# Output projection of a hybrid decoder block: two of its four column chunks in one seven-product block

## The reference

```
merged = sigmoid(ga) * y_attn + sigmoid(gc) * y_conv      # 256 x 2048
mix    = merged @ w_out                                   # w_out is 2048 x 2048
h      = layer_norm(DN_ALPHA * h + mix, ln2_g, ln2_b)
```

## Time and profile before

| | us |
|---|---|
| median of 3 runs | 2113.2 |
| lowest and highest run | 2110.99, 2113.87 |
| span of the profiled execution (first to last instruction) | 2109.5 |
| TensorE matmul busy | 2095.7 (99%) |
| VectorE busy | 1877.2 (89%) |
| ScalarE busy | 1402.9 (67%) |

### The profile page before, as it was taken

One profiled execution on the slowest core, in us unless ns is written; L12 is line 12 of the kernel. 1 busy time (PEld: TensorE's weight loads), 2 busy tenths in 40 slices (PEclk: granted clock), 3 DMA queues, 4 the chain that ended last, 5 costly groups with the idle time before them and its releaser, 6 DMA issues.

```text
span 2109.5 us, 23778 instructions
## 1 busy us (share of the span) xinstructions
PE 2095.7 (99%) x9386; PEld 1734.6 (82%) x9386; DVE 1877.2 (89%) x1420; ACT 1402.9 (67%) x1313; POOL 216.7 (10%) x345
## 2 busy tenths in 40 slices
PE   9999999999999999999999999999999999999998
PEld 7888888888888888888888888888888888888886
DVE  7899999999996889999999986659899999999996
ACT  6677777777775546766676445335677777777773
POOL 0111111101110001011100000000111111100110
PEclk9999999999999999999999999999999999999999
DMA  9798988888985759998898556755788988899892
GB/s 369 253 295 260 279 270 266 291 300 277 289 279 231 276 158 311 299 269 270 304 301 262 212 185 240 260 178 200 244 294 255 282 272 267 290 302 278 288 285 113
DMA packets 92397, 556.65 MB, mean 264 GB/s; under 512 B 13056, under 2 KB 13440, under 8 KB 35200
## 3 DMA queue, kind: packets, MB, share of 16 engines
q1 hardware_dynamic: 68544, 437.69, 54.7%
q0 software_dynamic: 23744, 117.46, 25.8%
HBM read 534.13 MB, written 20.97 MB: 263 GB/s over the span
## 4 chain that ended last, share of the span: by engine, by line
PE 88%; DVE 8%; DMA 2%; ACT 1%; issue 1%; SPq 0%; DVEq 0%; ACTq 0%
PE acc L2259 14%; PE acc L2261 14%; PE acc L2260 14%; PE tb L2259 12%; PE tb L2261 12%; PE tb L2260 12%; PE acc L2197 3%; PE acc L2199 3%; PE acc L2198 3%; DVE g_lo L1338 3%; DVE cacc L1777 3%; DMA g_raw<-in_groups 1%; PE tb L2245 1%; DVE w_lo L1315 1%; DVE g_raw L1346 1%
## 5 line engine op out<-in xcount | busy, mean ns | idle before, releaser
L1338 DVE TENSOR_TENSOR g_lo<-g_raw,g_hi 128x2048 fp32r<-128x2048 f32 x506 | 1147.6, 2286 | 120.4 <-ACT g_hi L817 119.8
L817 ACT ACTIVATE g_hi<-g_raw 128x2048 fp32r<-128x2048 f32 x506 | 964.4, 1916 | 319.8 <-DVE g_raw L1346 121.5
L2259 PE MATMUL acc<-g_hi,xF_hi 128*128 128x512 f32 x1184 | 464.3, 392 | 0.6 <-ACT acc L899 0.6
L2261 PE MATMUL acc<-g_hi,xF_lo 128*128 128x512 f32 x1184 | 461.1, 389 | 0.0
L2260 PE MATMUL acc<-g_lo,xF_hi 128*128 128x512 f32 x1184 | 460.7, 389 | 0.0
L2259 PE MATMUL tb<-g_hi,xF_hi 128*128 128x512 f32 x760 | 296.3, 390 | 0.3 <-DVE g_lo L1338 0.2
L2261 PE MATMUL tb<-g_hi,xF_lo 128*128 128x512 f32 x760 | 295.7, 389 | 0.0
L2260 PE MATMUL tb<-g_lo,xF_hi 128*128 128x512 f32 x760 | 295.7, 389 | 0.0
L1346 DVE TENSOR_TENSOR g_raw<-g_raw,g_raw 128x2048 f32<-128x2048 f32 x120 | 274.3, 2286 | 1.3
L2259 PEld LDWEIGHTS acc<-g_hi,xF_hi 128*128 128x128 f32 x1184 | 222.3, 188 | 46.8 <-ACT acc L899 1.0
L2261 PEld LDWEIGHTS acc<-g_hi,xF_lo 128*128 128x128 f32 x1184 | 222.2, 188 | 46.8
(11 more groups left out here) (180 smaller groups left out, 2307.7 us busy)
## 6 DMA issues: line engine op xcount, KB each, us to landing
g_raw<-in_groups SPq DMA_DIRECT2D x356, 1024.0 KB, 7.2
g_raw<-in_groups POOLq DMA_DIRECT2D x80, 1024.0 KB, 8.6
raw<-in_stream SPq DMA_DIRECT2D x80, 512.0 KB, 4.5
bounce<-h_sq POOLq DMA_DIRECT2D x40, 256.0 KB, 5.5
h_in<-bounce POOLq DMA_DIRECT2D x160, 64.0 KB, 2.6
ln_gb<-in_ln SPq DMA_DIRECT2D x6, 1024.0 KB, 6.6
g_raw<-in_groups SPq DMA_DIRECT2D x6, 512.0 KB, 9.7
res<-in_x_rows SPq DMA_DIRECT2D x1, 2048.0 KB, 16.6
```

The lines of the kernel that those rows point to most:

```text
L817: act.activation(g_hi[:, n % RING], source[:], ACT.Copy).then_inc(g_hi_ready, 1)
L1338: dve.tensor_tensor(g_lo[:, n % RING], source[:], f32(g_hi[:, n % RING]), ALU.subtract).then_inc(g_lo_ready, 1)
L2259: pe.matmul(bank, x_hi_ap, g_hi[:, n % RING, blk], start=begin, stop=False, skip_group_check=True)
L2261: return pe.matmul(bank, x_lo_ap, g_hi[:, n % RING, blk], start=False, stop=end, skip_group_check=True)
```

## The change

The output projection's four column chunks are handled in another form. Chunk 0 and chunk 3 stay plain; chunks 1 and 2 become one seven-product block between them (chunk 1 in the place of "u", chunk 2 in the place of "g"). All weights come as 1 MB groups through `g_raw`, in the same numbering as the rest of the kernel, and units remain only for the two projections ahead of it.

- The block has 14 product groups and no plain groups among them. T1a, T1b, T2a and T2b are made by VectorE; T3a, T3b, T4a and T4b by adding DMAs from GpSimd.
- The factor sums S1 to S4 are made from two raw quarters, which ScalarE now copies out of PSUM when column blocks 0 and 1 are transposed (`merged_hi`, c < 2, four more copies), and from two that are still in PSUM.
- The plain chunk 0 accumulates in banks 2 and 3 (Z and W of the block), chunk 3 as well. So P5a, which opens bank W, waits until VectorE has taken chunk 0 out of both banks (`plain_rows`).
- Seven `g_raw` places are in use in this stage, three of them new (8 to 10; 8 and 9 lie over the convolution's factors). The loads of the norm's gain and bias now wait for P7b, and the second feed-forward's first loads stand behind them in SyncE's queue.
- Rows of the pair: `u_rows` (scale and subtract, then add a bank) and `g_rows`; statistics of all chunks are taken while the last chunk runs.

The diff, cut to the tables, the orders of the engines and the new waits:

```diff
+OUT_PAIR = ("P1a", "P1b", "P5a", "P5b", "P6a", "P3a", "P6b", "P3b", "P7a", "P7b", "P2a", "P2b", "P4a", "P4b")
+OUT_LOADS = {"qa": "P4a", "qb": "P4b", "ra": "P7a", "rb": "P7b", "ua": "P3a", "ub": "P3b", "ga": "P2a", "gb": "P2b"}
...
+OUT_SUMS = ("T1a", "T1b", "T2a", "T2b")
+OUT_PLAIN = (0, 3)
+OUT_U, OUT_G = 1, 2
...
+    def output(self, n, sums):
+
+        self.begin["out"] = (n, len(self.order))
+        n = self.output_plain(n, 0)
+        self.number("out", 0, True)
+        for m, name in enumerate(OUT_PAIR):
+            self.at["out", 0, name] = n + m
+        for name, last in OUT_LOADS.items():
+            self.load_at["out", 0, name] = len(self.order)
+            matrix, p = WEIGHTS[name]
+            self.load("out", (OUT_G, OUT_U)["gu".index(matrix)] * COLS, p, self.at["out", 0, last])
...
+            if k == outs:
+                free = {x: n - 7 for n, x in enumerate((4, 5, 10, 0, 1, 8, 9))}
...
+            slot_free(KO, 4)
+            load_group(KO)
+            sp.wait_ge(tr_full, t_convt + 4)
+            load_group(KO + 1)
+            load_group(KO + 2)
+            sp.wait_ge(lo_ready, UNITS - 2)
+            load_group(KO + 3)
+            sp.wait_ge(lo_ready, UNITS)
+            load_group(KO + 4)
+            sp.wait_ge(unit_used, UNITS)
+            for k in range(KO + 5, K1):
+                load_group(k)
+            sp.wait_ge(g_used, G.at["out", 0, "P7b"] + 1)
             load_gb(1, ln_gb[1])
-            for k in range(K1, K1 + 2):
+            for k in range(K1, K2):
+                if k in G.behind_out:
+                    sp.wait_ge(g_used, N1)
...
+                split_loaded(f, g, "P1a", "qa")
+                split_loaded(f, g, "P1b", "qb")
+                factors_hi(f)
+                split_sum(f, g, "P5a", "qa", "T1a")
+                fork(f, g, acc[:, BY], acc[:, BX], "P1b")
+                split_sum(f, g, "P5b", "qb", "T1b")
+                split_sum(f, g, "P6a", "qa", "T2a")
+                split_loaded(f, g, "P3a", "ua")
+                act.wait_ge(acc_out[1], 2 * (u1_end + 1))
+                fork(f, g, acc[:, BZ], acc[:, BW], "P5b")
+                split_sum(f, g, "P6b", "qb", "T2b")
+                split_loaded(f, g, "P3b", "ub")
+                act.wait_ge(t3a_ready, 16 * BLOCKS)
+                split(f, g, "P7a", "ra")
+                act.wait_ge(t3b_ready, fulls(f, g))
+                split(f, g, "P7b", "rb")
+                save_out(0, "P6b")
+                split_loaded(f, g, "P2a", "ga")
+                split_loaded(f, g, "P2b", "gb")
+                save_out(1, "P7b")
+                act.wait_ge(t4a_ready, fulls(f, g))
+                split(f, g, "P4a", "qa")
+                act.wait_ge(t4b_ready, 16 * (BLOCKS + 1))
+                split(f, g, "P4b", "qb")
...
-            hi(mix_out, 0, 4, 5, 6, 7)
+            split_out(0, 2)
             merged_hi(3)
-            with act.Fori(1, ND) as i:
-                hi(mix_out, i, *range(UD))
+            split_out(0, 3)
+            out_pair()
+            for p in range(PIECES):
+                split_out(1, p)
...
+            def plain_rows(m, t):
+
+                if m and t == 0:
+                    dve.wait_ge(out_full, 1)
+                else:
+                    dve.wait_ge(g_used, G.first["out", m] + PIECES)
+                cols = slice(OUT_PLAIN[m] * COLS, (OUT_PLAIN[m] + 1) * COLS)
+                dve.scalar_tensor_tensor(out=res[:, t, cols], in0=res[:, t, cols], scalar=ALPHA, in1=acc[:, 2 + t],
+                                         op0=ALU.mult, op1=ALU.add).then_inc(acc_out[1], 1)
...
+                bank, n, behind = ((BZ, 2, "P3b"), (BW, 3, "P5b"))[t]
+                dve.wait_ge(forked, forks("out", 0, n))
+                dve.scalar_tensor_tensor(out=res[:, t, u_cols], in0=res[:, t, u_cols], scalar=ALPHA, in1=act_sb[:, t],
+                                         op0=ALU.mult, op1=ALU.subtract).then_inc(u_scaled, 1)
+                dve.wait_ge(g_used, G.at["out", 0, behind] + 1)
+                dve.wait_ge(u_scaled, t + 1)
+                dve.tensor_tensor(res[:, t, u_cols], res[:, t, u_cols], acc[:, bank], ALU.add).then_inc(out_rows, 1)
...
+                for n in range(4):
+                    factor_sum(f, n)
+                lo_group(f, g, "P1a", "qa")
+                load_done(f, g, "ra")
+                split_done(f, g, "P1a")
+                add(qa, qa, ra)
+                factor_lo(f, 0)
+                lo_group(f, g, "P1b", "qb")
+                load_done(f, g, "rb")
+                split_done(f, g, "P1b")
+                add(qb, qb, rb)
+                lo_group(f, g, "P5a", "qa")
+                factor_lo(f, 1)
+                factor_lo(f, 2)
+                load_done(f, g, "ua")
+                split_done(f, g, "P5a")
+                add(qa, qa, ua)
+                plain_rows(0, 0)
+                plain_rows(0, 1)
+                lo_group(f, g, "P5b", "qb")
+                factor_lo(f, 3)
+                lo_group(f, g, "P6a", "qa")
+                load_done(f, g, "ub")
+                split_done(f, g, "P5b")
+                add(qb, qb, ub)
+                lo_group(f, g, "P3a", "ua")
+                lo_group(f, g, "P6b", "qb")
+                lo_group(f, g, "P3b", "ub")
+                lo_group(f, g, "P7a", "ra")
+                lo_group(f, g, "P7b", "rb")
+                lo_group(f, g, "P2a", "ga")
+                u_rows(0)
+                lo_group(f, g, "P2b", "gb")
+                lo_group(f, g, "P4a", "qa")
+                u_rows(1)
+                lo_group(f, g, "P4b", "qb")
...
-            lo(mix_out, 0, 4, 5, 6, 7)
+            lo_out(0, 2)
             merged_lo(3)
+            lo_out(0, 3)
             dve.wait_ge(res_loaded, 48)
-            with dve.Fori(1, ND) as i:
-                rows_before(mix_out, i, u0_mix, lambda: lo(mix_out, i, 0, 1, 2, 3), lambda: None)
-                lo(mix_out, i, 4, 5, 6, 7)
+            out_pair()
+            lo_out(1, 0)
+            for t in range(TT):
+                plain_stats(0, t)
+            lo_out(1, 1)
+            g_rows(0)
+            lo_out(1, 2)
+            g_rows(1)
+            lo_out(1, 3)
+            for t in range(TT):
+                pair_stats(t + 1, t, OUT_U)
+            for t in range(TT):
+                pair_stats(t + 3, t, OUT_G)
...
+                pool.wait_ge(t_ready, G.sum_no[f, g, "T1a"])
+                add_from_hbm(f, g, "ra", "ua", t3a_ready)
+                pool.wait_ge(t_ready, G.sum_no[f, g, "T1b"])
+                add_from_hbm(f, g, "rb", "ub", t3b_ready)
+                pool.wait_ge(g_lo_ready, lo_count(G.at[f, g, "P6a"]))
+                add_from_hbm(f, g, "qa", "ga", t4a_ready)
+                pool.wait_ge(g_lo_ready, lo_count(G.at[f, g, "P6b"]))
+                add_from_hbm(f, g, "qb", "gb", t4b_ready)
...
+                pe.wait_ge(acc_out[0], 2 * u0_mix)
+                out_product("P1a", X, A11, 0, begin=True)
+                out_product("P1b", X, A11, 1)
+                pe.wait_ge(x_lo, made + 1)
+                pe.wait_ge(acc_out[1], 2 * (u1_end + 1))
+                out_product("P5a", W, S1, 0, begin=True)
+                out_product("P5b", W, S1, 1)
+                wait_fork(f, g, 0)
+                pe.wait_ge(x_lo, made + 3)
+                out_product("P6a", X, S2, 0)
+                wait_fork(f, g, 1)
+                pe.wait_ge(x_lo, made + 4)
+                out_product("P3a", Z, S4, 0)
+                out_product("P6b", X, S2, 1)
+                out_product("P3b", Z, S4, 1)
+                wait_fork(f, g, 2)
+                out_product("P7a", X, S3, 0)
+                out_product("P7b", X, S3, 1)
+                out_product("P2a", Y, A12, 0)
+                out_product("P2b", Y, A12, 1)
+                wait_fork(f, g, 3)
+                out_product("P4a", X, A22, 0)
+                out_product("P4b", X, A22, 1)
+
+            def last_out():
+
+                n = G.first["out", 1]
+                pe.wait_ge(out_rows, TT)
+                for t in range(TT):
+                    for p in range(PIECES):
+                        if t == 0:
+                            wait_lo(pe, n + p)
+                        hi_part, lo_part = out_piece(p, t)
+                        for blk in range(GK):
+                            mm = mm3(acc[:, 2 + t], hi_part[:, blk], lo_part[:, blk], n + p, blk, p == 0 and blk == 0,
+                                     p == PIECES - 1 and blk == GK - 1)
+                        if t == 1:
+                            mm.then_inc(g_used, 1)
+                            if p >= 2:
+                                turn_piece(p - 2, 10, b_ln2)
+                        elif p == PIECES - 1:
+                            mm.then_inc(out_full, 1)
+
+            out_pair()
+            last_out()
```

More of the change, by code:

```diff
@@ L201, in mixing, with output_plain @@
         return n, sums
+    def output(self, n, sums):
[8 more added lines that the diff above has]
```

(29 more changed lines are left out.)

176 lines of the change are left out of this document (97 added, 79 removed).

## The result

| | before | after |
|---|---|---|
| median of the runs (8 each) | 2112.6 us | 2117.25 us (predicted 2117.5) |
| lowest, highest | 2110.99, 2113.87 | 2115.08, 2118.85 |
| span of the profiled execution | 2109.5 us | 2114.4 us |

The ratio of after to before is 1.0022, with a 95% interval of 1.0013 to 1.0031: the changed kernel is slower by some 4.6 us (2.7 to 6.5 by the interval), although TensorE has 24 matmuls less to do.

What follows compares the result with a forecast made beforehand. Bound by TensorE's matmul count before, by VectorE's work after: waits 9.1 less 5.44 saved give +3.65 us, +4.26 with the clock's 0.6; 2113.2 + 4.3 = 2117.5 us. Range for 8 in 10: 2114.0 to 2121.5.

Steps and rivals of the forecast that it cites:

- TensorE saves 5.44: Chunks 1 and 2 of the output projection: 8 half products of 24 matmuls become 7, 5.44 us less for TensorE.
- VectorE's list to the release of the banks: VectorE's work from 11.4 until chunk 0's banks are free at 34.4 us; TensorE stands still 6.4 us at P5a.
- The wait is no price of its own: At P5a: without the bank wait, P5b's half still comes at 36.6 us, so the loss stays the same.
- First tile of the last chunk at 80.74: Last chunk: first tile full at 80.74 us against 77.1, +3.65; with the clock 81.35, +4.26.
- The clock, +0.6: After P5a's wait: twelve matmuls at 1.2 GHz cost 2.4 us, 1.8 absorbed, 0.6 reaching the end; bounds 0 and +1.4.
- Adding DMAs and ScalarE hidden: Whole stage: ScalarE's 51 us of 88 cost nothing except where named; no ScalarE wait for an adding DMA over 1 us.
- Rival 2: At P4b's weight sum: a late adding DMA delays the high half, 1.4 to 2.6 us more, 2119 to 2120.5; chance 0.12.
- VectorE is busy without a gap: Sign in the new profile: VectorE works unbroken for about 68 us from the first factor sum; idling would refute the forecast.
- Rival 1: Seven-product block: VectorE stays ahead if its list to the release takes under 16.8 us; only 5.44 counts, 2107.8; chance 0.05.
- No placing of waits makes it faster: Whole stage: VectorE becomes the owner in TensorE's place, so rearranging waits cannot shorten it.
- My second count: VectorE's work from 11.4 to the norm, without a schedule: 66.9 us, ending at 78.3, 1.0 over 77.3.
- a cause elsewhere: Sign of error: stage's and span's growth differing by over 1 us, first suspect the loads of the second feed-forward.

Runs made afterwards that it cites:

- Run 1: Changed kernel with VectorE's two additions that free chunk 0's banks placed directly behind P5a's low half, nothing added or removed; 2116.93 us, stage 92.82 us.
- Run 3: Changed kernel with 24 filler matmuls on TensorE between P1b and P5a, into a bank nobody reads; 2116.2 us, stage 92.58 us.
- run 6: On the changed kernel with chunk 0's fourth group and factor sum S3 made earlier, ScalarE seeds banks and takes chunk 0's rows from VectorE; 2109.42 us, stage 85.98.
- Run 4: Changed kernel with chunk 0's fourth group split ahead of merged block 3's halves on ScalarE and VectorE, same work; 2112.67 us, stage 89.46 us.

## Why the prediction came out right

The mechanism was right: TensorE is held up by VectorE's list at P5a and loses there more than the seven products save. That the number hit within 0.3 us is in part luck, as the last two points say.

- **TensorE saves 5.44.** 360 matmuls instead of 384 in the stage, at the same pitch.
- **VectorE's list to the release of the banks ends at 34.4; P5a waits 6.4.** Measured 34.4 and 6.38. The terms printed for that list add up to 23.1 and not 22.2: the 5.0 for the four factor sums already holds their meetings with each other's results. The slip and the 0.8 put on top of it cancel; the list took 23.1. The rows behind it agree likewise: low half of P6a 39.9 (39.95), P3a's 44.3 (44.35), P4b's 66.6 (66.7), last low half 77.8 (77.9).
- **The wait is no price of its own** ("without it ... the loss stays the same"). Run 1 shows it.
- **First tile of the last chunk at 80.74, +3.65 (81.35, +4.26 with the clock).** VectorE's row behind it starts at 1421.36, 81.05 into the stage, so it was full at about 80.85. The stage grew by 3.76. That the stage's length, 92.58, is close to the 92.7 forecast is partly an accident: the 88.5 that 4.2 were added to is 88.82 by the same measure.

```profile
1418.17 2.46 DVE L1773 BATCH_NORM_STATS2 stats<-res 128x6 f32<-128x512 f32 x4
1421.36 0.69 DVE L1738 SCALAR_TENSOR_TENSOR res<-res,acc 128x512 f32<-128x512 f32 x1 [0.73 <-PE acc L2436]
```

- **The clock, +0.6: mis-sized.** It fell, and nowhere else in the body of the span, but nine matmuls were slow and not twelve (1.8 us and not 2.4), and all of it was absorbed. Run 3 puts its price at 0.00. The lower bound given, 0 for eight matmuls at half clock, was the right value. Run 1, with 14 of them, shows where the cover ends: there the stage is 0.24 us longer. The row that the twelve were read from has a granted clock of 1.00, at odds with its own spacing of 0.42 to 0.43; in the changed kernel the same spacing stands at a granted clock of 0.50, so the reading of the spacing held.
- **Adding DMAs and ScalarE hidden.** ScalarE has no wait for a DMA in the stage; the four adding DMAs take 8.0 us (median). Rival 2 didn't come. ScalarE's only waits for a weight sum, 5.6 us in two, are for sums of VectorE.
- **"VectorE is busy without a gap", "I am wrong if VectorE idles within the block".** It does idle within the block, 1.67 us at P4a's half. The schedule of the prediction has this gap (58.9 to 60.9; measured 59.2 to 60.85), its list of signs forgot it. It can cost no more than the 0.5 us that TensorE loses at P4b:

```profile
1401.17 2.29 DVE L1434 TENSOR_TENSOR g_lo<-g_raw,g_hi 128x2048 fp32r<-128x2048 f32 x1 [1.67 <-ACT g_hi L872]
```

- **Rival 1, where "the cover holds".** Its threshold, the banks released in time, was too generous: in run 6 the banks are not waited for at all, and the stage still stands at 85.98 and not at 83.4 (88.82 less 5.44), mainly for the wait of 1.6 us at P3a. And one of its grounds isn't so: before the change, too, TensorE waits in the input projection, 0.6 us at 794.2, for ScalarE's copy of a bank.
- **"No placing of waits makes it faster"** held only for the list as it stands, counted from 11.4. That start was itself a matter of order: the list stood behind a step that ScalarE could give later. Run 4 took 3.12 us off by placing alone. My second count, 66.9 us of work, is about what VectorE did; its start wasn't a constant, and its end (78.3) is a lower bound that the changed kernel missed by 2.7 us.
- **The span grew by 4.9 and the stage by 3.76.** The prediction named a difference of over 1 us as a sign of a cause elsewhere. It is elsewhere, but not in the loads of the second feed-forward: the projection starts 1.17 us later (1340.31 against 1339.14). Of this 0.65 is there at TensorE's first matmul of queries and keys, behind a wait that differs from one execution to the next (last section), and 0.46 comes from a wait for VectorE near 1247, in the attention's output projection, with 1.52 us between two matmuls against 1.06 (1246.56 in the earlier trace rows):

```profile
1247.75 0.50 PE L2381 MATMUL acc<-w_hi,oT_hi 128*128 128x512 f32 x1 [1.14 <-DVE sig_a L2062]
```

In all eight changed kernels this distance is longer than in the one trace of the kernel before, 1.26 to 2.16 us. Whether the change causes that is not shown.
- **The number.** The forecast stood on a median of 2113.2 (three runs), which eight runs put at 2112.6, and added 4.3, where the medians differ by 4.65 and the stage by 3.76. The base was 0.6 too high and the growth of the stage 0.5; the 0.9 us by which the medians differ more than the stage were in no term, and make up for most of it. Of the 3.7 us between span and median that were taken as fixed, 1.8 to 1.9 lie around the span in every run on record; the other 1.8 to 1.9 came from a profiled execution that was quicker than the median.

## What to carry over

Count the work of the engine that feeds the bound engine, from the point where it can start to the point where it is needed, and compare that with the matmuls in between: fewer matmuls there are worth nothing as long as the supplier's list is the longer one (run 6, with a shorter list, got 2.84 of the 5.44 us). A wait at one place says little about its remedy: a wait that vanishes at one group comes back at the next if the list is unchanged, while starting the list earlier or shortening it pays one for one (3.1 for 3.1, 2.3 for 2.4, 1.2 for 1.2). Look for the list's first avoidable wait, and for idle time ahead of the stage where parts of it fit.
